# Rounding the second weight tile of each stage one stage ahead, and a retention layer with fewer block boundaries

## What is computed

```python
h = h + mixer(rmsnorm(h))          # RG-LRU + sliding window; retention; gated delta rule; dilated attention
h = h + (silu(n @ Wg) * (n @ Wu)) @ Wdown      # n = rmsnorm(h)

# the retention mixer, per head (4 heads, keys of 256, values of 512)
q, k, v, g = split(n @ w_in)                    # 1024, 1024, 2048, 2048 columns
q, k = rotary(q), rotary(k) * 256 ** -0.5
o = (q k^T * decay, causal) v
y = (silu(g) * rms_noaffine(o)) @ w_out
```

## Time and profile before

| | |
|---|---|
| runs | 3064.03, 3074.26, 3074.32 us; median 3074.26 |
| profiled execution | 3069.41 us |
| its span, first to last instruction | 3067.6 us |
| TensorE busy | 2941.2 us (96%) |
| VectorE, ScalarE, GpSimd busy | 1441.6, 1107.0, 85.8 us |
| mean granted TensorE clock | 0.979 |

### The profile page before, as it was taken

One profiled execution on the slowest core, in us unless ns is written; L12 is line 12 of the kernel. 1 busy time (PEld: TensorE's weight loads), 2 busy tenths in 40 slices (PEclk: granted clock), 3 DMA queues, 4 the chain that ended last, 5 costly groups with the idle time before them and its releaser, 6 DMA issues. The chain is left out here.

```text
span 3067.6 us, 39418 instructions
## 1 busy us (share of the span) xinstructions
PE 2941.2 (96%) x16406; PEld 2491.5 (81%) x16406; DVE 1441.6 (47%) x1613; ACT 1107.0 (36%) x1519; POOL 85.8 (3%) x92
## 2 busy tenths in 40 slices
PE   8999999999999899999998988999999999899999
PEld 8889999998976678888776787788887787778887
DVE  5664323334314544445475745544546755543322
ACT  5443332232232224331354534434223336443321
POOL 0000000003200000000000000000002000000000
PEclk9999999999999999999999999999999999899999
DMA  4112332223221235556421221455555221033322
GB/s 132 63 42 79 86 96 81 85 83 104 69 90 48 55 89 164 153 144 192 120 82 56 69 42 42 120 155 156 167 170 118 83 83 32 15 96 96 91 85 84
DMA packets 409377, 292.68 MB, mean 95 GB/s; under 512 B 24851, under 2 KB 388180, under 8 KB 409250
## 3 DMA queue, kind: packets, MB, share of 16 engines
q1 hardware_dynamic: 403210, 286.68, 32.0%
q0 software_dynamic: 1600, 3.55, 0.7%
q10 hardware_dynamic: 4440, 0.64, 0.2%
HBM read 286.16 MB, written 4.13 MB: 95 GB/s over the span
## 5 line engine op out<-in xcount | busy, mean ns | idle before, releaser
L197 DVE TENSOR_TENSOR w_lo<-w_raw,w_hi 128x2048 fp32r<-128x2048 f32 (+3 forms) x237 | 498.6, 2104 | 523.4 <-ACT w_hi L191 522.9
L191 ACT ACTIVATE w_hi<-w_raw 128x2048 fp32r<-128x2048 f32 (+3 forms) x237 | 416.2, 1756 | 261.7 <-PE ps L278 150.3
L276 PE MATMUL ps<-ffn_h_hi,w_hi 128*128 128x264 f32 (+1 forms) x1008 | 324.5, 322 | 3.1 <-DVE w_lo L197 3.1
L278 PE MATMUL ps<-ffn_h_hi,w_lo 128*128 128x264 f32 (+1 forms) x1008 | 323.8, 321 | 0.0
L277 PE MATMUL ps<-ffn_h_lo,w_hi 128*128 128x264 f32 (+1 forms) x1008 | 323.7, 321 | 0.0
L276 PE MATMUL ps<-up_act_hi,w_hi 128*128 128x512 f32 (+1 forms) x880 | 310.1, 352 | 0.1
L277 PE MATMUL ps<-up_act_lo,w_hi 128*128 128x512 f32 (+1 forms) x880 | 309.3, 351 | 0.0
L278 PE MATMUL ps<-up_act_hi,w_lo 128*128 128x512 f32 (+1 forms) x880 | 309.2, 351 | 0.0
L276 PE MATMUL ps<-up_h_hi,w_hi 128*128 128x512 f32 x672 | 265.8, 396 | 3.6 <-DVE w_lo L197 3.6
L278 PE MATMUL ps<-up_h_hi,w_lo 128*128 128x512 f32 x672 | 266.1, 396 | 0.0
L277 PE MATMUL ps<-up_h_lo,w_hi 128*128 128x512 f32 x672 | 265.8, 396 | 0.0
(11 more groups left out here) (581 smaller groups left out, 5623.1 us busy)
## 6 DMA issues: line engine op xcount, KB each, us to landing
mod_raw<-in_w_ada_dram SPq DMA_DIRECT2D x128, 384.0 KB, 3.7
w_raw<-in_ffn_w_gu_dram SPq DMA_DIRECT2D x88, 512.0 KB, 5.1
w_raw<-in_w_ffn_in_dram SPq DMA_DIRECT2D x88, 512.0 KB, 5.1
w_raw<-in_ret_w_in_dram SPq DMA_DIRECT2D x24, 1024.0 KB, 5.1
w_raw<-in_ffn_w_down_dram SPq DMA_DIRECT2D x32, 704.0 KB, 4.5
w_raw<-in_w_ffn_out_dram SPq DMA_DIRECT2D x32, 704.0 KB, 4.6
w_raw<-in_dsw_w_in_dram SPq DMA_DIRECT2D x18, 1024.0 KB, 4.9
w_raw<-in_gdn_w_in_dram SPq DMA_DIRECT2D x16, 1024.0 KB, 5.5
```

The source lines that it names most:

```text
L191: self.nc.scalar.activation(self.w_hi[:, s, 0:w.size], self.raw[:, s, 0:w.size], ACT.Copy).then_inc(self.hi_ready, 1)
L197: self.nc.vector.tensor_tensor(self.w_lo[:, s, 0:w.size], self.raw[:, s, 0:w.size], self.w_hi[:, s, 0:w.size].bitcast(F32), ALU.subtract). ...
L276: nc.tensor.matmul(out, w_hi, h_hi, start=first, stop=False)
L278: return nc.tensor.matmul(out, w_lo, h_hi, start=False, stop=last)
```

## The change

Second tiles: ScalarE makes the high half of the second tile at the end of the stage before (`two_ahead=True` wherever a normalized stage follows, and in the prologue for the first one), and GpSimd makes the low half, as the first instruction of the new block. VectorE and ScalarE leave that tile out in the new stage; before VectorE makes the third tile it waits for `lo_ready`. This is so in all eight stages that begin with a normalization: mixer, four feed-forward parts, retention keys, gated delta rule, dilated attention. In the delta rule the high half was made early before too, and VectorE's low half moves to GpSimd.

Retention inputs: keys, queries, values and gates are one block. `project` and `values_and_rotation` become classes with a method for each engine. The value tiles use PSUM banks 4, 5, 6 and 2, 3, 7 in turn in place of 0 to 2 and 4 to 6; the rotation waits for the last query eviction (`psum_free`), the tables' loads wait for the normalization, ScalarE waits for both rotations before the gates.

Retention heads and output: the total of head 2 stands behind the first of the four value groups of head 3; the total of head 3 stands in the output projection, ahead of row 6 of its first tile. The first two tiles of that projection go together: rows 0 to 11 of both, then rows 12 to 15 of both, each waited for alone. The second of them is rounded by ScalarE ahead of the last root and by GpSimd.

```diff
-    def split_lo(self, dve, w, i, j):
+    def split_lo(self, eng, w, i, j, on=None):
...
+    def second_of_next(self, w):
+        return self.after(w, w.trips - 1, w.unroll - 1, 2, True)
...
+class Project:
+    def gpsimd(self, pool):
+        if self.norm:
+            self.K.split_lo(pool, self.w, 0, 1, on=self.K.nc.gpsimd)
...
+    def vector(self, dve):
+        def trip(i, last, early=False):
+            for j in range(w.unroll):
+                if j and early:
+                    dve.wait_ge(K.lo_ready, K.tile_no(w, 0, 1) + 1)
+                if j or not early:
                     K.split_ahead(K.split_lo, dve, w, i, j, last)
+        K.over_tiles_peeled(dve, w, first, trip)
...
             if two_ahead:
-                K.split_hi(act, *K.after(w, w.trips - 1, w.unroll - 1, 2, True))
+                K.split_hi(act, *K.second_of_next(w))
...
-            if two_ahead:
-                K.split_lo(dve, *K.after(w, w.trips - 1, w.unroll - 1, 2, True))
...
+            def first_pair(i, last):
+                for k0, k1 in ((0, before.LATE), (before.LATE, w.rows)):
+                    for j in range(2):
+                        pe.wait_ge(K.lo_ready, K.tile_no(w, i, j) + 1)
+                        hi, lo = K.weights(w, j, K.w_hi), K.weights(w, j, K.w_lo)
+                        for k in range(k0, k1):
+                            if j == 0:
+                                before.row_ready(pe, k)
+                            at = slice(cols[0] - base, cols[0] - base + wd)
+                            mm = split_products(nc, K.ps[:, j, 0:wd], hi[:, k, 0:P], lo[:, k, 0:P], src[0][:, k, at],
+                                                src[1][:, k, at], k == 0, k == w.rows - 1)
+                        if k1 == w.rows:
+                            mm.then_inc(K.tile_used, 1)
...
-            project(K, W["ret_k"], k, ALL, norm=norm)
-            project(K, W["ret_q"], q, ONLY_X, base=N_META)
-            values_and_rotation(K, W["ret_v"], v, v_last, q, k, spare)
-            project(K, W["ret_g"], gate, ONLY_X, base=N_META, func=ACT.Silu)
+            keys = Project(K, W["ret_k"], k, ALL, norm=norm)
+            queries = Project(K, W["ret_q"], q, ONLY_X, base=N_META)
+            values = ValuesAndRotation(K, W["ret_v"], v, v_last, q, k, spare, norm)
+            gates = Project(K, W["ret_g"], gate, ONLY_X, base=N_META, func=ACT.Silu)
+            with K.nc.Block() as block:
...
+    LATE = NV * (RET_HEADS - 1)
+
     def row_ready(self, pe, row):
-        if row % self.NV == 0:
+        if row == self.LATE // 2:
+            self.total(pe, RET_HEADS - 1)
+        if row >= self.LATE:
+            pe.wait_ge(self.S["lo"], row + 1)
+        elif row % self.NV == 0:
             pe.wait_ge(self.S["lo"], row + self.NV)
...
     def gpsimd(self, pool):
         self.K.nc.gpsimd.memset(self.p_last[:], 0.0).then_inc(self.S["cleared"], 1)
+        self.K.split_lo(pool, self.w, 0, 1, on=self.K.nc.gpsimd)
...
-            if h:
-                total(h - 1)
+            if 0 < h < RET_HEADS - 1:
+                self.total(pe, h - 1)
             for m in range(NV):
                 e = h * NV + m
                 bank = 5 + e % 2
+                if m == 1 and h == RET_HEADS - 1:
+                    self.total(pe, h - 1)
...
-        total(RET_HEADS - 1)
...
+        K.split_hi(act, self.w, 0, 1)
         std(RET_HEADS - 1)
```

More of the change, by code:

```diff
@@ L448, in vector @@
         rest(*pieces[-1])
[L451 to L469, removed]
-                    K.split_ahead(K.split_hi, act, w, i, j, last)
[L471 to L484, removed]
-                    K.split_ahead(K.split_lo, dve, w, i, j, last)
[L486 to L519, removed]
@@ L588, in _ @@
                 K.over_tiles_unrolled(w, lambda i, last: side.loads(sp, w, i, last))
-        if before and not isinstance(before, Up):
+        if before:
             @block.gpsimd
@@ L1491, in scalar @@
         self.norm.scalar(act)
-        ahead(0)
         for c in range(2):
@@ L1626, in vector @@
         self.norm.vector(dve)
-        ahead(0)
         conv(0)
         conv(1)
+        dve.wait_ge(K.lo_ready, K.tile_no(*self.tiles[1]) + 1)
         ahead(1)
@@ new lines, in gpsimd, with tensor, trip @@
+    def gpsimd(self, pool):
+        K, nc = self.K, self.K.nc
+        nc.gpsimd.memset(self.v_last[:], 0.0).then_inc(self.cleared, 1)
+        pool.wait_ge(self.loaded, 32)
+        pool.wait_ge(K.psum_free, self.freed)
+        for dst, x, by, op in self.turns(self.k, 0, "k"):
+            K.pool.link(pool, nc.gpsimd.tensor_tensor(dst, x, by, op))
+        self.k_turned = (K.pool.sem, K.pool.n)
+    def tensor(self, pe):
+        K, nc, w = self.K, self.K.nc, self.w
+        def trip(i, last):
+            for j in range(w.unroll):
+                pe.wait_ge(K.lo_ready, K.tile_no(w, i, j) + 1)
+                pe.wait_ge(K.psum_free, i * w.unroll + (self.freed + j - 1))
+                hi, lo = K.weights(w, j, K.w_hi), K.weights(w, j, K.w_lo)
+                for b, (view, first, end) in enumerate(self.views):
+                    for c in range(w.rows):
+                        mm = split_products(nc, self.place(j, b, 0, end), view(K.h_hi, c), view(K.h_lo, c),
+                                            hi[:, c, :], lo[:, c, :], c == 0, c == w.rows - 1)
+                mm.then_inc(K.tile_used, 1)
+        K.over_tiles(pe, w, trip)
```

284 lines of the change are left out of this document (188 added, 96 removed).

## The result

The changed kernel takes 3076.27 us (median of 20 runs, 3072.34 to 3081.24), the kernel before 3068.88 us (20 runs, 3064.03 to 3074.32). The ratio is 1.0023, with a 95% interval of 1.0017 to 1.0029: slower by 7 us, a small loss and a real one. The profiled execution took 3073.94 us, against 3069.41 of the one that the prediction summed from.

What follows compares the result with a forecast made beforehand. TensorE, busy 96% of the span, was taken to bound the kernel. From the profiled 3069.4 us, 12 lost at the heads plus 4 of clock, less 7.8 and 4.5 gained in retention, gave 3073; range 3054 to 3086.

Steps and rivals of the forecast that it cites:

- seven heads, stall: Stage heads outside the delta rule: VectorE waits for GpSimd's split, so the second tile starts later; 10.5 us lost.
- seven heads, clock: Same heads: TensorE idles before the first low half and then gets a lower clock; 4 us lost, between nothing and 12.
- delta rule: Gated delta head: VectorE delayed 3.45 us by GpSimd's split, less 1.95 for an earlier start; 1.5 us lost.
- retention inputs: Keys to gates in one block: three boundaries' idle time and a slow clock behind the last vanish; 7.8 us gained.
- retention heads and projection: Moved totals and paired output tiles hide waits, though the third tile waits anew; 4.5 us gained, between 2 and 6.
- GpSimd holds VectorE: Stage heads: VectorE's first instruction with two SBUF inputs waits until GpSimd's 4.5 us split ends.
- Rival 1: Stage heads: GpSimd's split doesn't delay VectorE, so the waits for low halves are won; 3047 us, chance 0.12.
- rival 2: Seven heads: each loses a whole half-clock slice or two after the new idle time; 3081 to 3088 us, chance 0.12.
- Head 2's total: Last retention head: moving this total of squares behind the first product group gains 2.8 us.
- Rival 3: Retention part gives nothing: the third tile's wait and GpSimd's port eat the heads' gain; 3078 us, chance 0.10.
- About 0.5% is what a measurement tells: Whole kernel: the smallest difference that a measurement tells from no change, put at about 0.5% (15 us).
- the 8.0 us of the earlier trace: Six TensorE waits for late low halves of second tiles, 8.0 us in all, expected to vanish.

Runs made afterwards that it cites:

- e3: The changed kernel with nine extra matmuls per head, results unread, before TensorE's wait for the first low half at the seven heads: 3066.74 us.
- e1: The changed kernel with the second tile's low half made by VectorE behind its normalization, not by GpSimd, at the stage heads: 3047.04 us.
- e7: e1 with the total of head 2 again before the last head's first product group: 3046.84 us.
- e8: e1 with the output projection again tile by tile, the last total ahead of it, its second tile split in the stage: 3049.03 us.
- e4: The changed kernel without its retention parts (four input blocks, totals and output projection as before), split still on GpSimd: 3090.30 us.
- e12: e1 with the second tile's high half made in the stage again, at all heads but the delta rule's: 3049.12 us.

## Why the prediction came out as it did

The forecast was 3073.0, within 0.5% of before. The changed kernel's profiled execution took 3073.9, but its median is 3076.3, and 20 runs tell its 0.23% from nothing. So the call of no change that can be measured was wrong. The sign depends on the base. The sum started from the profiled 3069.4 and forecast some 3.7 us more; 20 runs give 3068.9 and 7.4 more. Against the median shown, 3074.3, of only three runs, 3073 was a small gain, and that sign was wrong. The range (3054 to 3086) holds the time. Term by term, in the profiled executions (us, + is slower):

| term | forecast | measured |
|---|---|---|
| seven heads, stall | +10.5 | +12.0 |
| seven heads, clock | +4 | +11.6 |
| delta rule | +1.5 | +1.2 |
| retention inputs | -7.8 | -8.1 |
| retention heads and projection | -4.5 | -3.2 |
| elsewhere | none | -9.0 |
| sum | +3.7 | +4.5 |

- **GpSimd holds VectorE: right, and to the size.** Split 4.53 (4.5 forecast), first low product 5.87 after the first `scale` (5.96). With the clock taken out (e3) the seven heads sum to 118.0, forecast 116.6; the stall is 12.0, forecast 10.5. Delta rule 1.2, forecast 1.5. Rival 1, with its 3047, is refuted by the trace; its world is e1, which takes 3047.
- **The clock: the step that failed.** I took 4 us, "since much of the slice will fall into the idle time itself". It measured 11.6 at the heads and 9.5 in the medians (changed kernel less e3). The stretches at half speed did not lie mostly in the idle time but behind it: the retention keys have 0.88 over 645.04 to 650.91, with the stall, and 0.80 over 650.91 to 664.15, where TensorE works without a pause; over the seven heads 32 of the 51 us lie behind. One row of before spoke for it, the 0.50 behind an idle time in the earlier trace rows; I used it for the rate and not for the place. With 11.6 the sum would have been 3080.7; rival 2's mechanism was right and its first size, 12 us, nearly so; but its time, 3081, was not reached, for the reason in the last but one point, and 3088 was too far.
- **Retention inputs: right.** 8.1 won in place, forecast 7.8.
- **Heads and projection: 3.2 won, forecast 4.5** and a range of 2 to 6. Head 2's total gives 2.5 in the changed kernel's trace and 2.0 between e7 and e1 (2.8 forecast). Counted from the heads' start it comes when it came before, so 2.75 of its wait are left, as the forecast implied. The third group waits 0.56 and not 2.4, since the second, partly at half speed, takes 4.3 us and not 2.45. The last total waits 1.08 (0.4 forecast) and the third tile 3.00 (3.1); behind that lie 3.4 us at half speed, 1.7 lost, for which I had taken off 1.4. The pairing gives 1.4 (e8). Rival 3, by its 3078 the loss of the 4.5 alone, is against the trace, which has 3.2, and against e4, where these parts are worth 4.2 in place.
- **What no step had:** the 6 to 9 us won far from the change. That the total still came within 1 us of the profiled execution, and 3.3 of the median, is luck: they hid most of the 9 us that the heads lose beyond the forecast. A trace is one draw of them, and their cause stays open.
- **"About 0.5% is what a measurement tells":** too wide. Five rounds tell 0.15%, 20 runs 0.06%.

## What to carry to other kernels

Before work is moved to GpSimd, look at what VectorE does at that moment: here a GpSimd instruction that reads SBUF held VectorE's instruction with two SBUF inputs until it ended (3.82 us instead of 0.43), so put it beside evictions from PSUM, or cut it in pieces of the length of VectorE's own instructions, or leave it on VectorE where its slack is. The stalls of 3 to 4 us here cost about half as much again in clock, most of it behind them (21 us of stall between e1's heads and e3's, 11.6 of clock on top); count both, and if the stall can't go, fill it with matmuls whose result isn't read (9.5 us here). Two stalls close together can cost more than their sum: in the traces here the one block was worth 9.5 us beside the head's stall and 5.9 without it.

## What the runs showed beside that

**ScalarE's function tables.** The change peels the first trip of ScalarE's loops, only to leave one split out. In the kernel before, ScalarE's groups of costly instructions had these (x count, busy us, mean ns):

```profile
L191 ACT ACT_TABLE_LOAD x43 | 55.2, 1283 | 3.5 <-DMA w_raw<-in_w_ffn_in_dram 1.5 <-PEq L1909 0.5 <-DMA w_raw<-in_ffn_w_gu_dram 0.4
L737 ACT ACT_TABLE_LOAD x40 | 51.3, 1283 | 0.7
```

In the changed kernel the first is gone and the second is

```profile
L783 ACT ACT_TABLE_LOAD x4 | 5.1, 1283 | 0.1
```

The trips of the feed-forward loops had loaded a table ahead of the high half and another ahead of the Silu; with a first trip ahead of the loop, one load a stage is left. Over the whole kernel 120 loads became 39, which is 104 of ScalarE's 108 us less. Most of it lay in ScalarE's idle time, but one load stood ahead of the second tile's high half at each feed-forward head, as in ScalarE's timeline of the kernel before:

```profile
254.41 1.28 ACT L191 ACT_TABLE_LOAD   x1
255.71 1.91 ACT L191 ACTIVATE w_hi<-w_raw 128x2048 fp32r<-128x2048 f32 x1
```

In e12 that load is gone, and the second tile starts 1.3 to 1.4 us sooner after the first `scale` than before the change at each of the four feed-forward heads, 5.5 us together. So a part of the 8.0 us of the earlier trace rows was this load. The Trainium skill, page ScalarE activation tables: per-element evaluation and per-set limits, section Table sets in the compiler and the runtime, says that the compiler's back end places the table loads per block. The traces fit that, with 83 loads at these two lines before and 4 after, but no run here takes it apart.

**Pieces on GpSimd.** 2048 columns took 4.53 us whole, 4.86 in two pieces and 6.42 in eight, probably in part because VectorE now takes its turns between them, which no run shows apart.

**Half speed is left over.** e1 still has some 100 us at the lower clock, 41 of them in the delta rule and 24 in dilated attention. How much of that can be had wasn't tried.
